# Two decoder layers on one core: normalisation ends written in halves, latent branch tiles first, weight splits inside the first routing unit

## The chip, the core and the metric

The kernel runs on one core of a Trainium2 chip. The metric is the device time in microseconds, the median of the runs. "Span" is the stretch from the first to the last instruction of one profiled execution. TensorE does matmuls into PSUM, VectorE and ScalarE work element by element, GpSimd (POOL) does a few such operations and starts small transfers, and SyncE (SP) starts the large ones.

## The reference, cut to what matters

The input is 256 tokens of width 1024. After an input LayerNorm come two layers:

```python
def hybrid_layer(x, ...):
    c_q, c_kv, k_r, n_q, n_kv, n_gate, m_gate = split(x @ w_in)
    y_mla = mla_attention(q, k, v from c_q, c_kv, k_r) @ w_branch_mla     # 8 heads, latent attention
    y_nsa = nsa_attention(compressed, selected, window) @ w_branch_nsa    # 8 heads in 2 groups
    g_mla, g_nsa = split(sigmoid(m_gate))
    mixed = (g_mla * y_mla + g_nsa * y_nsa) @ w_out
    x = layer_norm(ALPHA * x + mixed, ln1_g, ln1_b)
    x = layer_norm(ALPHA * x + peer(x, ...), ln2_g, ln2_b)
    return x

def peer(x, w_query, sub_keys, expert_u, expert_v):   # 8 heads, two sets of 128 keys, 16384 experts
    q = x @ w_query
    s = q . sub_keys                                   # 8 heads x 2 x 128 scores a token
    sv, si = top_k(s, 16)
    best, pos = top_k(sums of all pairs of sv, 16)     # 16 experts a head and token
    gate = softmax(best)
    return sum over them of gate * gelu(u_e . x) * v_e
```

The kernel computes gelu(u_e . x) for all 128 x 128 experts and multiplies it by a gate that is zero where an expert was not picked.

## The kernel before, in words

**Tiles and splits.** All weights stream through a ring of four slots of 512 KB: 68 tiles of the front part of a layer (T_LAT, T_UQ, T_B, T_UKV, T_MG, T_A, T_BR, T_OUT, T_PQ), 128 tiles of peer_u, 128 of peer_v. SyncE waits for `slot_free` and starts the load (L386, `load`). ScalarE writes the rounded `hi` part of a tile (L477, `split_hi`), VectorE the rest, `lo` (L734, `split_lo`), in place of the raw tile, three tiles ahead of TensorE (AHEAD). Products are made of three matmuls: lo by hi, hi by lo, hi by hi (L1245 to L1247 in `columns_tile`, L1256 in `rows_tile`, L1531 and on for the branch tiles). `tile_step(l, n)` on either engine is the split of tile n + 3.

**Order.** Each engine has its own instruction stream, written out by hand; semaphores order them. The two layers are a loop (`Fori(0, DEPTH)`) on every engine, and the u and v tiles, the query tiles and the gate groups are loops inside it.

**Ends of a sublayer.** `add_and_norm` on VectorE takes the two token tiles in turn: it adds the PSUM result (wide) to ALPHA x (L1067), forms the statistics (L748 to L750), gives the variance to GpSimd, which raises it to the power -1/2 (L427), multiplies (L756), and writes x (L761). TensorE's `transpose_x` (L1274) then transposes x in four groups, two for each token tile, into the two banks of `tr`; `transposed_hi` on ScalarE (L510) and `transposed_lo` on VectorE (L818) split each group. Groups 2 and 3 use the banks of groups 0 and 1 and wait until VectorE has read those. This happens at the start, after each w_out product (LN1), and at the border of the layers. The very first thing on VectorE is the arithmetic of the rotary angles (L768 to L784), whose sines ScalarE makes (L499, L500); after the input normalisation come eight copies into the cos and sin tables (L794 to L801), and four small constants.

**Attention.** Twelve units of four heads each: for each token tile two latent ones, and selected and window for both groups. TensorE runs the scores of unit u+1, a gate tile of the merge gates while there are any, the transposes of the weights of unit u (L1357), and the outputs of unit u-1 (L1504). Outputs go to one of two banks of `acc`, in the order of ATT_ORDER; `copy_o` (L591) and `output_lo` (L1014) split them.

**Branch tiles.** After the last output ScalarE makes four sigmoids of the gates (L631). The eight branch tiles alternate between the latent and the sparse branch for each quarter q of the columns. VectorE multiplies each by its gates (L1046), adds the two (L1054), ScalarE and VectorE split the sum (L638, L1035) into the input of the w_out tiles. Of the eight w_out tiles the last four run for token tile 0 first, then for token tile 1.

**Routing.** `route` is a chain of 14 stages (25 VectorE instructions, L1106 to L1131) that picks the experts of one of 16 units (token tile and head). The splits of the u tiles stand at fixed places in it (`split_after`). Unit 0 runs ahead of the loop with the split of one tile (T_U+3) in it; unit i+1 has the splits of eight tiles.

Of the kernel before, what the change touches and what calls it, by code (L numbers as in the profile page):

```python
# [22 lines left out]
F32 = mybir.dt.float32  # L23
# [9 lines left out]
P = 128  # L33
# [62 lines left out]
    0, 8, 10, 17, 19, 20, 24, 40, 48, 56, 60, 188)  # L96

ATT_ORDER = "F0 F1 O0 F2 O1 F3 O2 F4 F5 O3 F6 F7 O4 O5 O6 O7".split()
O_USE = [A_ATT + ATT_ORDER.index(f"O{k}") for k in range(8)]
MG_USE = [12, 13, 14, 15, 16, 18, 22, 23] + [A_ATT + ATT_ORDER.index(f"F{k}") for k in range(8)]  # L100
# [9 lines left out]
X_XT, X_Q, X_K, X_NQ, X_KT, X_CD, X_HT, X_PC, X_AT, X_XT2, X_PK = 0, 4, 8, 12, 14, 16, 18, 20, 24, 42, 46  # L110
NTR = 48
# [63 lines left out]
def build(nc, t, out):  # L175
    with ExitStack() as ctx:
# [24 lines left out]
        rot = at("rot", [P, TT, ROT, HD], F32, 48 * K)  # L201
        mix = at("mix", [P, 2, 2, 512], F32, 48 * K)
# [91 lines left out]
        ang = at("ang", [P, 4, TT, 48], F32, 0)  # L294
# [33 lines left out]
        x_ready = sem("x_ready")  # L328
        tr_hi = sem("tr_hi")
# [42 lines left out]
        def _(sp):  # L372
# [7 lines left out]
            def load(l, src, first, turns):  # L380
                with sp.Fori(0, turns) as q:
                    for s in range(SLOTS):
                        turn = l * TURNS + (q + first // SLOTS)

                        sp.wait_ge(slot_free[s], OPEN + turn)
                        sp.dma_start(raw[:, s], src[l, q * SLOTS + s]).then_inc(loaded[s], 16)  # L386

            with sp.Fori(0, DEPTH) as l:
                load(l, t["front"], 0, FRONT // SLOTS)
# [5 lines left out]
            sp.wait_ge(stored, 16)  # L395
# [3 lines left out]
        def _(pool):  # L399
# [31 lines left out]
            with pool.Fori(0, DEPTH) as l:  # L431
# [42 lines left out]
        def _(act):  # L474
# [23 lines left out]
            act.wait_ge(angles_ready, 1)  # L498
            nc.scalar.activation(ang[:, 2], ang[:, 0], ACT.Sin).then_inc(sines_ready, 1)  # L499
            nc.scalar.activation(ang[:, 3], ang[:, 1], ACT.Sin).then_inc(sines_ready, 1)  # L500

            with act.Fori(0, DEPTH) as l:
                warm_up(ACT.Gelu, l * 2 + 1)
                for n in range(AHEAD):
                    split_hi(l, 0, n)

                def transposed_hi(first, hi_first, dst):
                    for g in range(4):
                        act.wait_ge(tr_ready, l * NTR + first + g + 1)
                        nc.scalar.activation(dst(g), tr[:, (first + g) % 2].rearrange("p (c t) -> p c t", c=4),  # L510
                                             ACT.Identity).then_inc(tr_hi, 1)
# [5 lines left out]

                transposed_hi(X_XT, 0, xT_part)

# [93 lines left out]

                exp_scores(0)
                for u in range(NU + 1):
                    if u + 1 < NU:
                        exp_scores(u + 1)
# [9 lines left out]
                for b in range(2):  # L627
                    act.wait_ge(acc_read[b], OPEN + l * (NACC // 2) + A_BR // 2)
                g2 = gates[:].rearrange("p (b c) t -> p b c t", b=2)
                for q in range(4):  # L630
                    nc.scalar.activation(g2[:, :, 2 * q:2 * q + 2], g2[:, :, 2 * q:2 * q + 2],  # L631
                                         ACT.Sigmoid).then_inc(gates_ready, 1)
                for q in range(4):
                    for e in range(2):
                        tile_step(l, T_BR + 2 * q + e)
# [4 lines left out]
                for n in range(T_OUT, T_PQ):  # L640
                    tile_step(l, n)

                transposed_hi(X_XT2, 4, xT_part)
# [28 lines left out]
                with act.Fori(0, NKEYS // 8 - 1) as i:  # L672
# [3 lines left out]
                for e in range(8):  # L676
                    gelu_tile(NKEYS // 8 - 1, e)
                    if e == 1:
# [52 lines left out]
        def _(dve):  # L731
# [20 lines left out]
            def normalise(tt, nth, loads, chain, meanwhile=None):  # L752
# [14 lines left out]
            tab = Steps(dve, tables_step, 0, 19)  # L767
            dve.wait_ge(pos_loaded, 32)  # L768
            tab.link(nc.vector.tensor_copy(pos_f[:], pos_i[:]))
            for tt in range(TT):  # L770
                tab.link(nc.vector.tensor_scalar(ang[:, 0, tt], freq[:], pos_f[:, tt:tt + 1], None, ALU.mult))

            tab.link(nc.vector.tensor_scalar(ang[:, 1], ang[:, 0], 1.0 / TWO_PI, None, ALU.mult))
            tab.link(nc.vector.tensor_scalar(ang[:, 1], ang[:, 1], ROUND, None, ALU.add))
            tab.link(nc.vector.tensor_scalar(ang[:, 1], ang[:, 1], ROUND, None, ALU.subtract))
            for part in (PI_A, PI_B, PI_C):
                tab.link(nc.vector.scalar_tensor_tensor(out=ang[:, 0], in0=ang[:, 1], scalar=-part, in1=ang[:, 0],
                                                        op0=ALU.mult, op1=ALU.add))
            tab.link(nc.vector.tensor_scalar(ang[:, 0], ang[:, 0], float(np.float32(np.pi)),
                                             -float(np.float32(np.pi)), ALU.min, ALU.max))  # L780

            tab.link(nc.vector.scalar_tensor_tensor(out=ang[:, 1], in0=ang[:, 0], scalar=-1.0, in1=ang[:, 0],
                                                    op0=ALU.mult, op1=ALU.max))
            nc.vector.tensor_scalar(ang[:, 1], ang[:, 1], -1.0, float(np.pi / 2), ALU.mult, ALU.add).then_inc(angles_ready, 1)  # L784
# [6 lines left out]
            dve.wait_ge(sines_ready, 2)  # L791
            R2, H2 = ROPE // 2, HD // 2

            tab.link(nc.vector.tensor_copy(cos_m[:, :, :R2], ang[:, 3, :, :R2]))  # L794
            tab.link(nc.vector.tensor_copy(cos_m[:, :, R2:], ang[:, 3, :, :R2]))
            tab.link(nc.vector.tensor_copy(sin_m[:, :, R2:], ang[:, 2, :, :R2]))
            tab.link(nc.vector.tensor_scalar(sin_m[:, :, :R2], ang[:, 2, :, :R2], -1.0, None, ALU.mult))
            tab.link(nc.vector.tensor_copy(cos_n[:, :, :H2], ang[:, 3, :, R2:]))
            tab.link(nc.vector.tensor_copy(cos_n[:, :, H2:], ang[:, 3, :, R2:]))
            tab.link(nc.vector.tensor_copy(sin_n[:, :, H2:], ang[:, 2, :, R2:]))  # L800
            tab.link(nc.vector.tensor_scalar(sin_n[:, :, :H2], ang[:, 2, :, R2:], -1.0, None, ALU.mult))  # L801
            tab.end()
# [8 lines left out]
            with dve.Fori(0, DEPTH) as l:  # L811
                st = Steps(dve, dve_step, l * DVE_STEPS, DVE_STEPS)
                split_lo(l, 0, 0)
# [915 lines left out]
```

## Time and profile before

| | |
|---|---|
| median of 3 runs | 2300.91 us (2300.28 to 2303.41) |
| the profiled execution's own time | 2301.64 us |
| its span | 2300.0 us |
| TensorE busy | 2149.0 us, 93% |
| VectorE, ScalarE, GpSimd busy | 1507.9, 1161.5, 177.3 us |
| transfers | 353.47 MB, mean 154 GB/s |
| granted TensorE clock, mean | 0.975 |

In the page's matmul groups durations overlap, since matmuls are pipelined: a 128x256 matmul of 285 ns starts 0.12 us after the one before it. What an engine waited for stands in brackets behind its row, as the idle time before it and what ended that. "issue" there means that the profile shows nothing that released it.

### The profile page before, as it was taken

The numbers are of one execution on the slowest core, as the hardware profiler recorded it, in microseconds if no ns is written. First come the engines' busy times: TensorE is split into PE (matmuls) and PEld (weight loads), VectorE is DVE, ScalarE is ACT, GpSimd is POOL, SyncE is SP. The second block draws the span as 40 slices with busy tenths as digits, with TensorE's granted clock in tenths as the row PEclk, the third lists the DMA queues.
The fourth block names the chain that finished last, engine by engine and source line by source line (L and its number), as shares of the span: only waits on it lengthen the run. The fifth ranks groups of instructions, "written<-read, shape, count | busy, mean of one in ns | idle before, by whom it ended". The sixth has DMA issues, their size and how long they took to land.

```text
span 2300.0 us, 42749 instructions
## 1 busy us (share of the span) xinstructions
PE 2149.0 (93%) x14160; PEld 1928.2 (84%) x14160; DVE 1507.9 (66%) x2784; ACT 1161.5 (50%) x1830; POOL 177.3 (8%) x188
## 2 busy tenths in 40 slices
PE   6988979999999999999988888899999999999997
PEld 5876779999997788788777767899999977887886
DVE  5656657777777855555557557577777687555555
ACT  4445444555557745444444454455545587545543
POOL 2000000000005600000020000000000074000000
PEclk9999989999999999999989999999999999999999
DMA  4622434555551065655546214355555501565554
GB/s 157 226 77 65 154 121 163 181 182 182 181 183 59 13 195 193 196 194 194 169 155 212 76 63 146 130 183 181 182 182 182 174 28 60 193 210 178 194 195 139
DMA packets 96309, 353.47 MB, mean 154 GB/s; under 512 B 11056, under 2 KB 11088, under 8 KB 95856
## 3 DMA queue, kind: packets, MB, share of 16 engines
q1 hardware_dynamic: 94032, 341.90, 45.2%
q0 software_dynamic: 2208, 10.66, 1.4%
q8 instruction: 42, 0.69, 0.1%
q14 instruction: 27, 0.22, 0.0%
HBM read 351.47 MB, written 1.05 MB: 153 GB/s over the span
## 4 chain that ended last, share of the span: by engine, by line
PE 58%; issue 28%; DVE 6%; ACT 4%; POOL 2%; DMA 2%; POOLq 0%; DVEq 0%; ACTq 0%; SPq 0%
PE wide L1256 14%; PE acc L1245 12%; PE acc L1246 12%; PE acc L1247 12%; PE acc L1618 3%; POOL hot_i L463 1%; ACT sc L607 1%; DMA raw<-in_front 1%; ACT hot_i L693 1%; DVE lo L734 1%; ACT hi L477 1%; DVE negmax L987 1%; PE tr L1357 1%; POOL rstd L427 1%; PE acc L1504 1%
## 5 line engine op out<-in xcount | busy, mean ns | idle before, releaser
L734 DVE TENSOR_TENSOR lo<-raw,hi 128x1024 fp32r<-128x1024 f32 x648 | 792.2, 1223 | 589.3 <-ACT hi L477 584.5
L477 ACT ACTIVATE hi<-raw 128x1024 fp32r<-128x1024 f32 x648 | 686.7, 1060 | 520.4 <-DMA raw<-in_peer_v 354.4
L1245 PE MATMUL acc<-xT_hi,lo 128*128 128x256 f32 x2560 | 734.7, 287 | 27.2 <-DVE lo L734 11.2
L1246 PE MATMUL acc<-xT_lo,hi 128*128 128x256 f32 x2560 | 731.1, 286 | 0.0
L1247 PE MATMUL acc<-xT_hi,hi 128*128 128x256 f32 x2560 | 730.8, 285 | 0.0
L1245 PEld LDWEIGHTS acc<-xT_hi,lo 128*128 128x128 f32 x2560 | 498.6, 195 | 32.9 <-DVE lo L734 18.2
L1246 PEld LDWEIGHTS acc<-xT_lo,hi 128*128 128x128 f32 x2560 | 498.7, 195 | 0.1
L1247 PEld LDWEIGHTS acc<-xT_hi,hi 128*128 128x128 f32 x2560 | 498.4, 195 | 0.0
L1256 PE MATMUL wide<-hi,w_lo 128*128 128x512 f32 x1024 | 318.7, 393 | 12.0 <-DVE w_lo L1202 12.0
L1256 PE MATMUL wide<-lo,w_hi 128*128 128x512 f32 x1024 | 316.8, 391 | 0.0
L1256 PE MATMUL wide<-hi,w_hi 128*128 128x512 f32 x1024 | 316.4, 391 | 0.0
L665 ACT ACTIVATE big<-acc 128x256 f32 (+1 forms) x256 | 98.6, 385 | 345.5 <-PE acc L1247 345.5
L1256 PEld LDWEIGHTS wide<-hi,w_lo 128*128 128x128 f32 x1024 | 192.8, 189 | 54.5 <-DVE lo L734 10.9
L1256 PEld LDWEIGHTS wide<-lo,w_hi 128*128 128x128 f32 x1024 | 193.6, 189 | 40.9
L1256 PEld LDWEIGHTS wide<-hi,w_hi 128*128 128x128 f32 x1024 | 193.1, 189 | 40.2
L463 POOL TENSOR_TENSOR hot_i<-iota,picksT 128x512 f32<-128x512 f32 x128 | 133.1, 1041 | 866.3 <-PE acc L1247 835.3
L1618 PEld LDWEIGHTS acc<-hot_j,hot_i 128*128 128x128 f32 x1024 | 128.2, 196 | 38.1 <-ACT hot_i L693 27.8
L1618 PE MATMUL acc<-hot_j,hot_i 128*128 128x128 f32 x1024 | 145.6, 287 | 10.5 <-ACT hot_i L693 8.3
L1202 DVE TENSOR_TENSOR w_lo<-big,w_hi 128x256 fp32r<-128x256 f32 x256 | 106.8, 418 | 1.1 <-ACT w_hi L713 1.1
L713 ACT ACTIVATE w_hi<-big 128x256 fp32r (+1 forms) x256 | 102.2, 400 | 2.7 <-DVE big L1185 2.7
L1185 DVE TENSOR_TENSOR big<-acc,big 128x512 f32 (+1 forms) x128 | 87.6, 684 | 14.5 <-PE acc L1618 13.6
L693 ACT ACTIVATE hot_i<-hot_i,ones 128x512 f32<-128x512 f32 x128 | 90.2, 706 | 0.0
(259 smaller groups left out, 1790.0 us busy)
## 6 DMA issues: line engine op xcount, KB each, us to landing
raw<-in_peer_u SPq DMA_DIRECT2D x256, 512.0 KB, 3.3
raw<-in_peer_v SPq DMA_DIRECT2D x256, 512.0 KB, 3.3
raw<-in_front SPq DMA_DIRECT2D x136, 512.0 KB, 3.6
ln_par<-in_ln POOLq DMA_DIRECT2D x10, 512.0 KB, 5.8
w<-in_cmp_w POOLq DMA_DIRECT2D x2, 2048.0 KB, 8.9
xs<-in_x SPq DMA_DIRECT2D x2, 512.0 KB, 7.2
keys<-in_sub_keys POOLq DMA_DIRECT2D x2, 512.0 KB, 4.0
out<-xs SPq DMA_DIRECT2D x1, 1024.0 KB, 3.9
```

The lines of the kernel that those rows point to most:

```text
L463: nc.gpsimd.tensor_tensor(hot_i[:, e], iota[:].unsqueeze(1).broadcast_to([P, 4, P]), toks, ALU.subtract).then_inc(differences_ready, 1)
L477: nc.scalar.activation(hi[:, s], raw[:, s], ACT.Identity).then_inc(hi_done, 1)
L665: nc.scalar.activation(big[:, i * 2 + e // JB, :, e % JB], acc[:, e % 2, :SEQ].rearrange("p (g t) -> p g t", t=TB), ACT.Gelu).then_inc(acc ...
L693: nc.scalar.activation(hot_i[:, e], hot_i[:, e], ACT.Relu, bias=ones[:, 0:1], scale=-1.0).then_inc(hot_i_ready, 1)
L713: nc.scalar.activation(w_hi[:, s].rearrange("p (g t) -> p g t", t=TB), big[:, i + c // JB, :, c % JB], ACT.Identity).then_inc(w_hi_done, 1)
L734: nc.vector.tensor_tensor(lo[:, s], raw[:, s], hi[:, s].bitcast(F32), ALU.subtract).then_inc(lo_done, 1)
L1202: nc.vector.tensor_tensor(w_lo[:, s].rearrange("p (g t) -> p g t", t=TB), big[:, i + c // JB, :, c % JB], part, ALU.subtract).then_inc(w_l ...
L1245: mm(dst, lo[:, s, c], xh[:, k], start=k == 0, stop=False)
L1246: mm(dst, hi[:, s, c], xl[:, k], start=False, stop=False)
L1247: ins = mm(dst, hi[:, s, c], xh[:, k], start=False, stop=k == DK - 1)
L1256: ins = mm(wide[:, tt, 512 * h:512 * h + width], a[:, tok], w[:, s, off:off + width], start=first and k == 0, stop=last and k == 2)
L1618: ins = mm(acc[:, e % 2, r * P:(r + 1) * P], hot_i[:, e, r], hot_j[:, e, r], start=True, stop=True)
```

## The change

On all engines the loop over the layers is written out (`for l in range(DEPTH)`). The edits, in order of the kernel:

- The first token tile's groups still go to `tr`; the second's go to `wide[:, 0]`, under two new semaphores. x is written in two halves, each with its own signal, and each group is transposed from its half. In `add_and_norm` the lo part of group 0 stands between the two steps of the second token tile's normalisation; at the border of the layers too.
- The angle arithmetic moves from VectorE's start to behind the first three splits of layer 0, and the table copies behind the third split of the query projection. The input is the first thing that VectorE works on.
- The output is stored in three parts: token tile 0, and the two halves of token tile 1.
- The branch tiles come as four latent ones (`y_mla` holds their gated results) and four sparse ones; the first latent one stands inside the last attention unit, ahead of its transposes. ScalarE makes the sigmoids in four steps around the last unit.
- In the routing the split of T_U+3 stands ahead of unit 0, and those of T_U+4 and T_U+5 inside it; the later units' splits move on by two tiles, and so do the steps at the end of the u tiles.

```diff
-ATT_ORDER = "F0 F1 O0 F2 O1 F3 O2 F4 F5 O3 F6 F7 O4 O5 O6 O7".split()
+ATT_ORDER = "F0 F1 O0 F2 O1 F3 O2 F4 F5 O3 F6 F7 O4 O5 O6 M0 O7".split()
...
-            sp.wait_ge(x_ready, TT * (1 + 2 * DEPTH))
-            sp.dma_start(out, xs[:]).then_inc(stored, 16)
+            sp.wait_ge(x_ready, last + 2)
+            sp.dma_start(out[:, 0], xs[:, 0]).then_inc(stored, 16)
+            for c in range(2):
+                sp.wait_ge(x_ready, last + 2 + c + 1)
+                sp.dma_start(out[:, 1, 512 * c:512 * c + 512], xs[:, 1, 512 * c:512 * c + 512]).then_inc(stored, 16)
...
@@ ScalarE
+                    if u == NU - 1:
+                        branch_gates(0)
+                    if u == NU:
+                        branch_gates(1)
+                        tile_step(l, T_BR)
...
+                branch_gates(2)
+                branch_gates(3)
+                for c in range(1, 4):
+                    tile_step(l, T_BR + c)
                 for q in range(4):
+                    tile_step(l, T_BR + 4 + q)
                     act.wait_ge(mix_sum, l * 4 + q + 1)
...
@@ VectorE
-                nc.vector.scalar_tensor_tensor(out=xs[:, tt], in0=xs[:, tt], scalar=rstd[:, tt:tt + 1],
-                                               in1=ln_par[:, 1], op0=ALU.mult, op1=ALU.add).then_inc(x_ready, 1)
+                for c in range(2):
+                    half = slice(512 * c, 512 * c + 512)
+                    nc.vector.scalar_tensor_tensor(out=xs[:, tt, half], in0=xs[:, tt, half], scalar=rstd[:, tt:tt + 1],
+                                                   in1=ln_par[:, 1, half], op0=ALU.mult, op1=ALU.add).then_inc(x_ready, 1)
...
+                branch_out(0, y_mla[:, 0])
                 output_lo(7)
+                for c in range(1, 4):
+                    branch_out(c, y_mla[:, c])
...
                 for q in range(4):
+                    branch_out(4 + q, mix[:, q % 2, 1])
+                    if q > 0:
+                        mixed_lo(q - 1)
+                    nc.vector.tensor_tensor(mix[:, q % 2, 0], y_mla[:, q], mix[:, q % 2, 1], ALU.add).then_inc(mix_sum, 1)
...
-                add_and_norm(0, T_PQ - 1, W_OUT, R_LN1, l * 64 + 64, lambda: tile_step(l, T_PQ - AHEAD))
-                transposed_lo(X_XT2, 4, x_part(xT_hi), x_part(xT_lo))
+                add_and_norm(0, T_PQ - 1, W_OUT, R_LN1, l * 64 + 64, lambda: transposed_lo(l, 1, 0))
+                transposed_lo(l, 1, 1)
+                tile_step(l, T_PQ - AHEAD)
+                transposed_lo(l, 1, 2)
+                transposed_lo(l, 1, 3)
...
-                route(0, 0, range(1))
+                after_route(0, 0)
+                route(0, 0, (1, 2))
                 with dve.Fori(0, NKEYS // 8 - 1) as i:
-                    route(i + 1, i, range(1, 9))
+                    route(i + 1, i, range(3, 11))
...
@@ TensorE
                     if u + 1 < NU:
                         scores(u + 1)
+                    else:
+                        outputs_read(4)
+                        outputs_read(5)
+                        branch_tile(0)
...
                 outputs(NU - 1)
...
+                for c in range(1, N_BR):
+                    if c == 4:
+                        outputs_read(6)
+                        outputs_read(7)
+                    branch_tile(c)
```

`branch_out(c, dst)` on VectorE waits for tile c and its gates, writes the product to dst and splits tile c + 3 of the branch tiles; `outputs_read(k)` waits until VectorE has split output k; `branch_tile(c)` is the old body of 24 matmuls.

## Rows read from the trace of the kernel before

**Rows 1.** The page's part 1: busy time, share of the span, instructions.

```profile
PE 2149.0 (93%) x14160; PEld 1928.2 (84%) x14160; DVE 1507.9 (66%) x2784; ACT 1161.5 (50%) x1830; POOL 177.3 (8%) x188
```

**Rows 2.** TensorE's waits: who waited <- for whom: us, times, longest.

```profile
PE tr L1274 <- DVE xT_lo L818: 28.2, 4, 8.6
...
PE acc L1245 <- DVE lo L734: 11.2, 2, 5.6
```

**Rows 3.** Timeline, the start: start us, duration us, instruction [idle before <- releaser].

```profile
18.60 0.17 DVE L794 COPY cos_m<-ang 128x32 f32<-128x32 f32 x1
...
20.91 1.22 DVE L734 TENSOR_TENSOR lo<-raw,hi 128x1024 fp32r<-128x1024 f32 x1
22.04 1.28 DVE L818 TENSOR_TENSOR xT_lo<-tr,xT_hi 128x512 fp32r<-128x512 f32 x2
...
26.44 0.58 PE L1245 MATMUL acc<-xT_hi,lo 128*128 128x256 f32 x1 [1.69 <-DVE xT_lo L818]
```

**Rows 4.** Timeline, LN1 of layer 0.

```profile
290.71 1.23 DVE L734 TENSOR_TENSOR lo<-raw,hi 128x1024 fp32r<-128x1024 f32 x1
...
295.57 0.69 DVE L818 TENSOR_TENSOR xT_lo<-tr,xT_hi 128x512 fp32r<-128x512 f32 x1 [1.24 <-ACT xT_hi L510]
...
297.69 0.58 PE L1245 MATMUL acc<-xT_hi,lo 128*128 128x256 f32 x1 [1.94 <-DVE xT_lo L818]
```

**Rows 5.** Timeline, the border of the layers.

```profile
1156.08 1.52 POOL L427 TENSOR_TENSOR rstd<-var,neg_half 128x1 f32<-128x1 f32 x1 [4.62 <-DVE var L754]
...
1160.82 1.22 DVE L734 TENSOR_TENSOR lo<-raw,hi 128x1024 fp32r<-128x1024 f32 x1 [1.90 <-issue]
...
1166.37 0.58 PE L1245 MATMUL acc<-xT_hi,lo 128*128 128x256 f32 x1 [1.70 <-DVE xT_lo L818]
```

**Rows 6.** Transfers by line: count, KB each, median us from issue to landing.

```profile
raw<-in_front SPq DMA_DIRECT2D x136, 512.0 KB, 3.6
...
out<-xs SPq DMA_DIRECT2D x1, 1024.0 KB, 3.9
...
lat_g<-in_lat_g POOLq DMA_DIRECT2D x2, 4.0 KB, 2.1
```

**Rows 7.** Timeline, the last attention unit of layer 0 and the first branch tile.

```profile
231.95 1.06 PE L1357 MATMUL tr<-ident,sc 128*128 128x128 f32 x8 [3.10 <-DVE sc L1000]
...
238.00 1.28 ACT L631 ACT_TABLE_LOAD   x1 [0.54 <-DVE oT_lo L1014]
238.11 0.38 PE L1531 MATMUL acc<-oT_hi,lo 128*128 128x256 f32 x1 [1.07 <-issue]
239.29 3.90 ACT L631 ACTIVATE gates<-gates 128x1024 f32<-128x1024 f32 x4
```

**Rows 8.** Windows: busy us by engine; then granted clock, DMA share, GB/s.

```profile
136.00:139.50 3.50, 3.50 (x34) 3.46 (x33) 0.99 (x1) 0.19 (x1) 0.00 (x0) 1.00 0.12 47
234.00:237.00 3.00, 3.00 (x16) 1.29 (x12) 0.00 (x0) 0.00 (x0) 0.00 (x0) 0.50 0.00 0
937.00:940.60 3.60, 3.60 (x11) 2.81 (x10) 3.55 (x6) 1.91 (x4) 0.00 (x0) 0.54 0.02 9
```

**Rows 9.** Timeline, branch and w_out tiles of layer 0.

```profile
264.96 0.68 DVE L1054 TENSOR_TENSOR mix<-mix 128x512 f32<-128x512 f32 x1
...
267.29 1.22 DVE L734 TENSOR_TENSOR lo<-raw,hi 128x1024 fp32r<-128x1024 f32 x1 [1.65 <-ACT hi L477]
...
278.36 0.72 PE L1256 MATMUL wide<-hi,xT_lo 128*128 128x512 f32 x2 [1.25 <-DVE lo L734]
```

**Rows 10.** Timeline of the first routing unit, and a window behind it.

```profile
329.67 0.29 DVE L1106 COPY r_s<-scr 128x256 f32<-128x256 f32 x1 [0.27 <-DVE scr L1083]
...
344.72 1.20 DVE L734 TENSOR_TENSOR lo<-raw,hi 128x1024 fp32r<-128x1024 f32 x1
...
345.98 0.58 PE L1245 MATMUL acc<-xT_hi,lo 128*128 128x256 f32 x1 [5.62 <-DVE lo L734]
...
346.00:349.60 3.60, 3.60 (x17) 3.60 (x18) 3.45 (x16) 0.00 (x0) 0.00 (x0) 0.50 0.02 5
```

More of the change, by code:

```diff
@@ L378, in _, with load @@
                 sp.dma_start(xs[:, tt], t["x"][:, tt]).then_inc(x_loaded[tt], 16)
-            def load(l, src, first, turns):
+            def load(l, src, first, turns, skip=0):
                 with sp.Fori(0, turns) as q:
@@ L430, in _ @@
                 rsqrt(tt, tt, tt + 1)
-            with pool.Fori(0, DEPTH) as l:
+            for l in range(DEPTH):
                 pool.wait_ge(slot_free[SLOTS - 1], OPEN + l * TURNS)
@@ L497, in _, with transposed_hi @@
             nc.scalar.activation(causal_r[:], causal[:], ACT.Identity).then_inc(masks_ready, 1)
[L498 to L502, printed above, removed]
+            for l in range(DEPTH):
                 warm_up(ACT.Gelu, l * 2 + 1)
[L504 to L510, printed above, removed]
+                def transposed_hi(first, tt, dst):
+                    for cg in range(2):
+                        if tt == 0:
+                            act.wait_ge(tr_ready, l * NTR + first + cg + 1)
+                            src = tr[:, cg]
+                        else:
+                            act.wait_ge(wide_x_ready, l * 4 + (2 if first == X_XT2 else 0) + cg + 1)
+                            src = wide[:, 0, 512 * cg:512 * cg + 512]
+                        nc.scalar.activation(dst(2 * tt + cg), src.rearrange("p (c t) -> p c t", c=4),
                                              ACT.Identity).then_inc(tr_hi, 1)
@@ L670, in after_gelu @@
                     split_hi(l, (i * 2 + n // SLOTS), n % SLOTS)
-                with act.Fori(0, NKEYS // 8 - 1) as i:
+                after_gelu(0, 0)
+                for e in range(8):
+                    gelu_tile(0, e)
+                    if e > 0:
+                        after_gelu(0, e)
+                with act.Fori(1, NKEYS // 8 - 1) as i:
                     for e in range(8):
@@ L1133, in route @@
                     assert sum(map(len, stages)) == ROUTE_STEPS
-                    split_after = [round((len(stages) - 1) * (e + 0.5) / 8) for e in range(8)]
+                    split_after = [round((len(stages) - 1) * (e + 0.5) / len(splits)) for e in range(len(splits))]
                     for g, stage in enumerate(stages):
@@ L1217, in _ @@
                 split_w_lo(0, NKEYS - 1, SLOTS - 1)
-                add_and_norm(1, NT - 1, W_V, R_LN2, l * 64 + 96)
+                add_and_norm(1, NT - 1, W_V, R_LN2, l * 64 + 96,
+                             (lambda: transposed_lo(l + 1, 0, 0)) if l + 1 < DEPTH else None)
                 st.end()
@@ L1506, in outputs, with branch_tile, outputs_read @@
                         ins.then_inc(acc_ready, 1)
+                def branch_tile(c):
+                    n, bank = T_BR + c, BR_USE[c] % 2
+                    s = n % SLOTS
+                    acc_free(l, BR_USE[c])
+                    tile_ready(l, n // SLOTS, s)
+                    for f in range(2):
+                        for k in range(4):
+                            w = slice(k * 256 + f * P, k * 256 + f * P + P)
+                            dst = acc[:, bank, f * SEQ:(f + 1) * SEQ]
+                            mm(dst, lo[:, s, w], oT_hi[:, c // 4, k], start=k == 0, stop=False)
+                            mm(dst, hi[:, s, w], oT_lo[:, c // 4, k], start=False, stop=False)
+                            ins = mm(dst, hi[:, s, w], oT_hi[:, c // 4, k], start=False, stop=k == 3)
+                    ins.then_inc(slot_free[s], 1)
+                def outputs_read(oi):
+                    use = O_USE[oi]
+                    pe_.wait_ge(acc_read[use % 2], OPEN + l * (NACC // 2) + use // 2 + 1)
                 scores(0)
@@ L1511, in _ @@
                         scores(u + 1)
+                    else:
+                        outputs_read(4)
+                        outputs_read(5)
+                        branch_tile(0)
                     if u + 8 < N_MG:
```

224 lines of the change are left out of this document (117 added, 107 removed).

## The prediction

> **What bounds the kernel now.** I read the page first: TensorE is busy 93% of the span [rows 1], so time can only come out of its idle stretches, or of stretches at half clock. The table of waits names the idle ones: the largest is TensorE's transposes of x held by VectorE's xT_lo (28.2 us in 4 waits), and two waits of 5.6 us for a weight split make up the 11.2 us of L1245 on L734 [rows 2]. Then I went through the timeline stage by stage: the start, the two ends of the mixing sublayer (LN1), the border of the layers, the last attention unit, the branch tiles, the first routing unit, the end. In each the reader is to see what VectorE does while TensorE waits, since that engine writes what TensorE waits for. The long loops over u and v tiles show no such waits and the change leaves them as they are.
>
> **Part 1, the normalisation ends.** The change gives the second token tile's transposes their own PSUM banks (wide), so they no longer wait until VectorE has read the first tile's; it moves the lo parts of the first token tile ahead; and it writes x in halves.
>
> *Start.* Before, the 8 table copies run from 18.60 to 20.37, then 4 small constants, a split at 20.91, two xT_lo from 22.04, then a hole until the second tile's transposes and hi parts come, two more xT_lo, and the first real matmul at 26.44 [rows 3]. After, the copies are gone from here (1.8) and the hole closes, because the second tile's transposes run while VectorE works on the first. VectorE then does, from the end of the second normalisation (18.67, earlier by up to 0.4 as the angle arithmetic no longer stands ahead of the statistics; I take 0.2): constants 0.55, two lo parts 1.28, a split 1.13, two lo parts 1.28, and TensorE starts 0.3 later: 18.5+0.55+1.28+1.13+1.28+0.3 = 23.0. Gain 3.4. The angle arithmetic (3.1 us of VectorE) now stands behind the first splits, beside the first weight tile, which takes 5.5 us at the start; if it were late, ScalarE's squares would slip and the spare accumulator bank gives 2.9 us more. The table copies move into the query projection, where the splits feed TensorE closely: I charge 0.3 (0 to 1.8). Net 3.1.
>
> *LN1, two layers.* Before: split at 290.71, then x, then four lo parts with a hole of 1.24 between them, the matmul at 297.69 [rows 4]. After, VectorE has no hole: lo part from 290.71 (0.60), two half writes 1.24, a lo part 0.60, the split 1.14, two lo parts 1.25, and the 0.6 to the matmul as before: 296.15. Gain 1.5 each, 3.0.
>
> *Border of the layers.* Before, after the loop's jump VectorE has 1.90 us of idle time that nothing releases, then the split at 1160.82, and the matmul comes at 1166.37 [rows 5]. After, with the layers written out, no jump; the first lo part fills the wait for rstd (ready at 1157.60 [rows 5]): x written 1158.0 to 1159.2, lo 0.6, split 1.14, two lo 1.25, 0.35: 1162.6. Gain 3.8.
>
> Rule of the Trainium skill beside it: "Runtime: NRT & Kernel Launch", section Instruction fetch mechanics, says that instructions are prefetched only straight ahead and that a taken branch to a page outside the window waits for a fetch. The 1.90 us agrees; by that rule nothing else is lost in writing out, and the sum stays.
>
> *The end.* One 1 MB store lands 3.9 us after its issue; a 4 KB transfer takes 2.1 [rows 6]. The last store after the change is 256 KB: a quarter of the way between, about 2.6. Gain 1.3 (0 to 1.8).
>
> Sum of part 1: 3.1+3.0+3.8+1.3 = 11.2.
>
> **Part 2, the branch tiles.** Before, TensorE idles 3.10 us ahead of the last unit's transposes (3.32 in layer 1), and the first branch tile starts at 238.11, 1.07 after the last output matmul, because it waits for that output's lo part [rows 7]. A branch tile is 24 matmuls at 0.12, 2.88 us. The one put inside the last unit fits the hole: its weights were split long before (by 214), its bank is free and the two outputs that it reads are done. The next three need only the latent branch, so the 1.07 goes too.
>
> The hole also costs afterwards. TensorE's granted clock is 0.50 from 233.8 to 237.1 (a row of [rows 8]), that is 1.2 instead of 2.4 GHz, just behind the 3.1 us of idle; it happens in both layers. All output matmuls of the last two units lie in it and take twice the time. With the hole filled I expect full clock: 3.0 us become 1.5. Both ends for this: 0 if the clock falls all the same, 1.6 if not. I take 1.5, since elsewhere TensorE at full work keeps 1.00.
>
> ScalarE must now load the sigmoid's table and do one gate before its share of pT: load 1.28, gate 0.98 (3.90 for 4) [rows 7], from 230.9 to 233.2; its pT copy then ends at 233.8 instead of 233.2. The outputs of unit 11 start after 234.4. Hidden. The Trainium skill, "ScalarE: Activation LUTs", section What ACT_TABLE_LOAD costs, adds a drain of about 1.4 us to each load; by it the copy would end at 235.1 and some 0.7 us per layer would be lost; here the sigmoid starts 1.29 after its load, so the sum goes without.
>
> So tile 1 starts at about 235.5, tile 4 ends at 247.0 (call it t).
>
> What is late next: the second half. The four sparse tiles come every 2.88, but each needs from VectorE a product, a split, a lo part and a sum, and these hang in one chain with ScalarE: from a sum at 264.96 over ScalarE's hi part and split to VectorE's split at 267.29 [rows 9] are 2.33, then 1.14 for it (the spacing of a split and what follows [rows 3]), 0.61 for the lo part, and the next sum: 4.08 a round. Before there was one round for two tiles (5.76). The first sum waits for the split of the tile whose slot tile 3 frees at t-2.9: load 3.6 [rows 6] with some waiting 3.8, hi 1.06, lo 1.13, so t+3.1; the fourth sum is t+15.3, and the split behind it, for output tile 3, is ready 3.5 later, t+18.8, where TensorE wants it at t+16.8. The loss is 2.1. Output tile 7 follows 8.9 behind tile 3, as before (269.4 to 278.36), since its slot comes free by tile 3: t+27.9 = 274.9 against 278.36 [rows 9]. Gain 3.45; in layer 1 the half-clock stretch is 0.3 shorter and the same sum gives 3.2. Part 2: 6.65. The bounds: with loads of 4.6 us (the longest here) 1 less per layer, without the clock's share 1.5 less.
>
> **Part 3, the first routing unit.** Before, route 0 runs from 329.67 to 343.6 with a single split in it; the second comes at 344.72 and TensorE idles 5.62 us until 345.98, then runs at 0.50 until 349.8, which costs another 2 [rows 10]. After: split of u tile 3 at 330.4 to 331.5; stages 0 to 3, 3.0; split of tile 4, ready 337.6 (wanted 340.4); stages 4 to 10, 4.7; split of tile 5, ready 343.5 (wanted 343.2, late 0.3); stages 11 to 13 and the first two of unit 1, 3.8; split of tile 6, ready 348.4 (wanted 346.4, late 2.0). From then on each split comes in time, as the steady loop has 17 us of VectorE work in 23. Stall 2.3 instead of 5.6: gain 3.3 a layer, 6.6. Behind a wait of 2 us in the v loop the clock was down for 3.6 us too [rows 8], so I leave the clock's 2 us as they are; if the clock stays up, 2 more per layer. The tail runs two tiles later against TensorE but keeps its order; the picks are copied some 7 us before they are wanted: nothing.
>
> **Sum.** 11.2+6.65+6.6 = 24.4 us off the profiled execution's 2301.64 (span 2300.0 and 1.64 around it): 2277.2. The median before is 0.7 lower than that execution: 2276.5.
>
> **Rivals.**
> 1. *Clock stays down in the last unit* and the chain of sums is as long as computed: 3.0 less, and longer loads 1 more: gain 20.5, 2280. For it: the clock fell in the v loop as well, behind a wait of 2 us and with TensorE at full work [rows 8]. Against it: the half clock of 234 to 237 has no other cause in sight. Chance 0.17.
> 2. *Clock stays up in the routing stage*, the stall being shorter: 4.0 more, 2272.5. For it: behind the wait of 2.3 us at 134 it stayed at 1.00 [rows 8]. Against: in the v loop it did not. Chance 0.22.
> 3. *Covered elsewhere:* TensorE's earlier work runs into loads, since the ring of 4 slots ties each split to the release 6 us before it; part 2 gives nothing and part 1 half: gain 12, 2289. Against it: DMA share is 0.5 and the loads are tied to releases, which move along. Chance 0.07.
> 4. *Slower:* writing both layers out makes each engine stream more distinct code, and a stream that runs dry costs what the jump costs now, 1.90 us. It decides from 13 such misses on the path; with 20 the time is 2301+38-24 = 2315. Against it: the layer's straight code is already streamed twice, with no unexplained stall but the one. Chance 0.03.
> The forecast has 0.51.
>
> **Range and chances.** 2270 to 2284 takes in the forecast, rivals 1 and 2 and the unknown ends above. A measurement of this kernel tells 0.2% (4.6 us) from no change: faster 0.94, same 0.03, slower 0.03.
>
> **What would show it.** First weight matmul at about 23; 1.5 between LN1's old and new place; no idle "issue" at VectorE at the border; a branch tile ahead of the last unit's transposes, granted clock 1.00 over them and the outputs; waits of TensorE for splits of about 2 us at output tiles 2 and 3; in the first routing unit a wait of about 2 us at tile 6 and none of 5.6. I am wrong if new idle of TensorE appears where none was, or if the time is above 2290.

## The result, and the profile after

The changed kernel takes 2270.74 us (median of 4 runs, 2268.11 to 2280.07) where the kernel before takes 2301.26 beside it (2300.28 to 2303.41). The ratio is 0.9879, 95% interval 0.9855 to 0.9903: 30.5 us less by the medians. The forecast was 2276.5, 24.4 less, with a range of 2270 to 2284. Direction and range held; the middle was 5.8 too high, and the time lies 0.7 above the low end of the range. The same kernel timed once more, as the control below, takes 2268.16, just under it. The profiled execution took 2271.67 us.

The page of the changed kernel, span and busy time (before: [rows 1]):

```profile
span 2269.9 us, 41699 instructions
...
PE 2145.3 (95%) x14160; PEld 1926.3 (85%) x14160; DVE 1509.6 (67%) x2794; ACT 1160.2 (51%) x1829; POOL 172.4 (8%) x188
```

TensorE's busy time is only 3.7 us lower; 26 of the 30 us came out of its idle time. Its waits (who waited <- for whom: us, times, longest):

```profile
PE wide L1337 <- DVE xs L802: 18.0, 4, 5.1
...
PE wide L1312 <- DVE lo L773: 10.3, 9, 2.0
PE acc L1695 <- ACT hot_i L732: 7.6, 2, 3.8
...
PE acc L1301 <- DVE lo L773: 3.6, 4, 1.6
```

Of the 28.2 us on xT_lo [rows 2] the first row is what is left (the second tile's transposes wait for x itself), and the 11.2 us of the routing unit's split are 3.6. The second row is mostly w_out tiles that wait for their splits. The third, the first gate group of each layer, waited 3.88 us before as well and was no part of the prediction; it comes back below.

**Where the 30.1 us of span came from.** I laid TensorE's rows of both traces side by side. The same matmul starts earlier after the change, and by how much is what has been gained up to there; what this grows by from one matmul to a later one is what the stretch between them gave.

| stretch | forecast | measured |
|---|---|---|
| start, to the first weight matmul | 3.4 | 3.6 |
| branch tiles, layers 0 and 1, from the last but two unit's transposes | 3.45, 3.2 | 2.6, 3.5 |
| LN1, two layers (1.4 in layer 0, layer 1 taken as the same) | 3.0 | 2.8 |
| routing, layers 0 and 1, first score matmul to the first gate matmul | 3.3, 3.3 | 5.3, 5.1 |
| border of the layers | 3.8 | 3.9 |
| end | 1.3 | 1.5 |
| all other stages together | -0.3 | 1.8 |

The last row is what is left of larger pieces, none of them forecast. The v loops gave 3.7 and 2.45, where stretches of half clock at 936.9 and 2073.5 (3.4 us long each) have no counterpart after the change and the waits ahead of them are shorter. The stages from the border to the last but two unit of layer 1 took 4.5 back, with 10.2 us more at half clock. That these nearly cancel is luck. In layer 1 the LN1 stretch by itself gave 0.6 in this trace, as half clock lies at its head; in the kernel with part 1 alone it gave 1.4 in both layers.

The start, LN1, the border and the end, on the timeline (start us, duration us, instruction [idle before <- releaser]; compare [rows 3 to 5]):

```profile
22.88 0.55 PE L1301 MATMUL acc<-xT_hi,lo 128*128 128x256 f32 x1 [2.91 <-issue]
...
284.04 0.69 DVE L831 TENSOR_TENSOR xT_lo<-tr,xT_hi 128x512 fp32r<-128x512 f32 x1
284.64 1.40 DVE L802 SCALAR_TENSOR_TENSOR xs<-xs,rstd,ln_par 128x512 f32<-128x512 f32 x2
...
286.57 1.21 DVE L773 TENSOR_TENSOR lo<-raw,hi 128x1024 fp32r<-128x1024 f32 x1
...
289.58 0.57 PE L1301 MATMUL acc<-xT_hi,lo 128*128 128x256 f32 x1 [2.17 <-DVE xT_lo L831]
...
1143.32 1.97 PE L1337 MATMUL wide<-ident,xs 128*128 128x128 f32 x8 [5.05 <-DVE xs L802]
...
1147.06 0.55 PE L1301 MATMUL acc<-xT_hi,lo 128*128 128x256 f32 x1 [1.77 <-issue]
```

The reader is to see that VectorE has no hole left between the first lo part and the matmul, neither in LN1 nor at the border. The stores (the page's part 6; us from issue to landing): the last two, half a token tile each, land 2.2 us after their issue, where the interpolation said 2.6:

```profile
out<-xs SPq DMA_DIRECT2D x1, 512.0 KB, 2.6
out<-xs SPq DMA_DIRECT2D x2, 256.0 KB, 2.2
```

The last attention unit of layer 0 (compare [rows 7]), then a window over it (us; busy by engine; granted clock, DMA share, GB/s):

```profile
226.10 1.28 ACT L638 ACT_TABLE_LOAD   x1
227.40 1.06 ACT L638 ACTIVATE gates<-gates 128x1024 f32<-128x1024 f32 x1
227.67 1.03 PE L1421 MATMUL tr<-ident,sc 128*128 128x128 f32 x8
...
234.26 0.69 DVE L1068 TENSOR_TENSOR y_mla<-acc,gates 128x512 f32<-128x512 f32 x1 [1.84 <-PE acc L1584]
```

```profile
230.00:237.00 7.00, 7.00 (x61) 6.40 (x58) 3.41 (x5) 4.05 (x5) 1.04 (x2) 1.00 0.60 241
```

The first sigmoid starts 1.30 after its table load does, as the one before the change had 1.29, and pT (ScalarE's copy of the transposed weights, which the outputs read) is in time. (The Trainium skill, "ScalarE: Activation LUTs", section What ACT_TABLE_LOAD costs, adds a drain of 1.4 us to the 1.28; the trace doesn't agree: neither the first ACTIVATE behind the load nor the load itself, which starts 0.02 behind the instruction ahead of it, shows such a time.) The transposes wait for nothing, and the outputs run at a granted clock of 1.00, the 2.4 GHz level, where [rows 8] had 0.50. Behind it the chain of sums, with TensorE's waits for the w_out splits:

```profile
246.75 0.68 DVE L1105 TENSOR_TENSOR mix<-y_mla,mix 128x512 f32<-128x512 f32 x1
...
250.82 0.68 DVE L1105 TENSOR_TENSOR mix<-y_mla,mix 128x512 f32<-128x512 f32 x1
...
254.90 0.68 DVE L1105 TENSOR_TENSOR mix<-y_mla,mix 128x512 f32<-128x512 f32 x1
...
258.60 0.70 PE L1312 MATMUL wide<-hi,xT_lo 128*128 128x512 f32 x2 [1.07 <-DVE lo L773]
258.97 0.68 DVE L1105 TENSOR_TENSOR mix<-y_mla,mix 128x512 f32<-128x512 f32 x1
...
262.67 0.70 PE L1312 MATMUL wide<-hi,xT_lo 128*128 128x512 f32 x2 [1.07 <-DVE lo L773]
...
271.65 0.70 PE L1312 MATMUL wide<-hi,xT_lo 128*128 128x512 f32 x2 [1.91 <-DVE lo L773]
```

The sums are 4.08 us apart, three times: the round of the forecast to the second decimal. Their matmuls belong to w_out tiles 2, 3 and 7. Last, the first routing unit (compare [rows 10]) and a window from 334 to 356, of the changed kernel and then of the kernel before:

```profile
336.07 0.39 PE L1301 MATMUL acc<-xT_hi,lo 128*128 128x256 f32 x1 [0.24 <-DVE lo L773]
...
340.76 0.39 PE L1301 MATMUL acc<-xT_hi,lo 128*128 128x256 f32 x1 [1.56 <-DVE lo L773]
...
334.00:356.00 22.00, 20.20 (x167) 19.80 (x166) 18.73 (x49) 9.65 (x14) 0.00 (x0) 1.00 0.50 168
```

```profile
334.00:356.00 22.00, 16.39 (x123) 16.18 (x122) 17.96 (x62) 7.11 (x10) 0.00 (x0) 0.84 0.38 121
```

The stall of 5.62 us is now waits of 0.24 and 1.56, and the clock stays at 1.00. The forecast had kept the half clock.

### The profile page after: what moved, and what is told of

Its sections match the earlier page's. It is cut to its first block, busy times and chain, and to the rows that moved or that the text cites. A ratio compares the mean times of both kernels' runs of the same rounds, so it can differ in the third digit from the quotient of the medians.

```text
span 2269.9 us, 41699 instructions
## 1 busy us (share of the span) xinstructions
PE 2145.3 (95%) x14160; PEld 1926.3 (85%) x14160; DVE 1509.6 (67%) x2794; ACT 1160.2 (51%) x1829; POOL 172.4 (8%) x188
## 4 chain that ended last, share of the span: by engine, by line
PE 80%; DVE 8%; ACT 4%; DMA 3%; issue 3%; POOL 1%; POOLq 0%; DVEq 0%; ACTq 0%; SPq 0%
PE wide L1312 33%; PE acc L1301 13%; PE acc L1302 12%; PE acc L1303 12%; PE acc L1695 4%; DVE lo L773 2%; DMA raw<-in_front 2%; ACT hi L491 1%; ACT sc L628 1%; DMA raw<-in_peer_v 1%; POOL hot_i L477 1%; PE wide L1664 1%; DVE negmax L1032 1%; DMA raw<-in_peer_u 1%; ACT hot_i L732 1%
## 5 line engine op out<-in xcount | busy, mean ns | idle before, releaser
L1232 DVE SCALAR_TENSOR_TENSOR hot_j<-wide,picksT 128x512 f32<-128x512 f32 x128 | 86.6, 679 | 6.2 <-PE acc L1303 6.2
```

## The experiments

Each was timed in five rounds against the kernel before, on the same chip. Ratios are to that, with their 95% interval; 0.001 is 2.3 us. Each letter in the expectations names one explanation and the time that it would give.

**One part at a time: the loops over the layers.** The kernel before with one edit on every engine:

```diff
-            with dve.Fori(0, DEPTH) as l:
+            for l in range(DEPTH):
```

> Kernel before with only the loop over the two layers written out on all engines. Theory A (each part of the change gains at its own place, and what came on top of the forecast is stretches of half clock that fell away): 1.9 us less at the border of the layers, where VectorE waited 1.90 us for nothing that the profile shows, so 2299.4 against 2301.3. Rival B (writing out is what gave the 6 us on top, as constants take the place of register sums ahead of each wait): 2293 to 2295.

Measured: 2295.8 us (2291.04 to 2299.0), ratio 0.998 (0.9968 to 0.9992), 2 to 7 us less. The border of its trace, against [rows 5]:

```profile
1151.69 1.28 DVE L761 SCALAR_TENSOR_TENSOR xs<-xs,rstd,ln_par 128x1024 f32<-128x1024 f32 x1 [0.52 <-POOL rstd L427]
1152.89 1.22 DVE L734 TENSOR_TENSOR lo<-raw,hi 128x1024 fp32r<-128x1024 f32 x1
...
1158.26 0.55 PE L1245 MATMUL acc<-xT_hi,lo 128*128 128x256 f32 x1 [1.46 <-DVE xT_lo L818]
```

The 1.90 us of "issue" between x and the split are gone. From the last wait of the v loop to this matmul it takes 19.4 us, before 21.5: the border gave 2.1. The Trainium skill, "Runtime: NRT & Kernel Launch", section Instruction fetch mechanics, says that a taken branch out of the prefetched code waits for a fetch. The trace fits it, in that the 1.90 us are gone with the jump; a fetch itself is not shown. The other 6.0 us of its profiled execution had been gained by then in stages without such a jump: two half-clock stretches of the trace of before, at 90 to 94 and 936 to 941, are missing here, 1.7 us each, and the v loop's first wait is 0.85 us instead of 2.06; 1.4 stay without a place. So the size lies nearer B, but for a reason that neither theory had.

**The routing alone.** The kernel before with the splits of the first unit as in the change:

```diff
-                route(0, 0, range(1))
+                after_route(0, 0)
+                route(0, 0, (1, 2))
```

> Kernel before with the routing edit alone (the split of u tile 3 ahead of unit 0, those of tiles 4 and 5 inside it, the later ones moved on). Theory A: two waits of 5.6 us become 0.3 and 1.6 in each layer, and no half clock follows, which gave 2 us: 2 x 5.3 = 10.6 less, 2290.7. Rival C (the clock staying up in the changed kernel was luck of where the stretch fell): 2 x 3.3 = 6.6 less, 2294.7, with a granted clock of 0.50 for some 4 us behind the wait of 1.6 us.

Measured: 2291.84 us (2287.98 to 2292.42), ratio 0.995 (0.9937 to 0.9962), 9 to 15 us less; the forecast for this part was 6.6. From the first score matmul of the routing to the first gate matmul, layer 0, it takes 388.7 us in the kernel before, 388.8, 388.7 and 389.0 in the three experiments that keep the old splits (layers written out, branch tiles alone, part 1 alone), 383.3 here and 383.4 in the changed kernel. Its window:

```profile
334.00:356.00 22.00, 20.26 (x167) 19.85 (x166) 17.75 (x55) 9.55 (x14) 0.00 (x0) 1.00 0.48 165
```

The clock is up here as well. So the 5.3 us belong to this part whatever else is in the kernel. Of the stall 3.8 are gone in the changed kernel (5.62 less 0.24 and 1.56); the rest, 1.5, I put down to the clock.

**The branch tiles alone.** The kernel before with the new order, the sigmoids and M0 in the last unit:

```diff
-ATT_ORDER = "F0 F1 O0 F2 O1 F3 O2 F4 F5 O3 F6 F7 O4 O5 O6 O7".split()
+ATT_ORDER = "F0 F1 O0 F2 O1 F3 O2 F4 F5 O3 F6 F7 O4 O5 O6 M0 O7".split()
```

> Kernel before with the branch edit alone (latent tiles first, one ahead of the last unit's transposes). Theory A: 2.9 for the tile in the hole, 1.1 for the wait before the first tile, 1.5 for the clock, less about 3 for the chain of sums: 2.4 to 3.4 a layer, 5 to 7 in all, 2294 to 2296, granted clock 1.00 over the last unit's outputs. Rival C: the half clock behind the hole stays: 2297 to 2299.

Measured: 2296.05 us (2285.68 to 2298.5), ratio 0.996 (0.9944 to 0.9977), 5 to 13 us less, forecast 6.65. In its trace the stretch from the last but two unit's transposes to the matmul behind LN1 is 2.8 us shorter than before in layer 0 and 4.3 in layer 1. The median is A's and the ratio is below both, and in both layers no half clock follows the last unit's transposes, so C, the clock staying down, is refuted by the trace. The runs spread by 13 us, so the times alone would not settle it.

**The hole left open.** The changed kernel with M0 behind the outputs of the last unit:

```diff
-                    else:
-                        outputs_read(4)
-                        outputs_read(5)
-                        branch_tile(0)
...
-                for c in range(1, N_BR):
+                for c in range(N_BR):
```

> Changed kernel with the first latent tile behind the last unit's outputs again, all else as changed. Theory A: the hole of 3.1 us comes back and with it a stretch of 0.50 of the clock over the outputs; 2.9 and 1.5 us lost in each layer: 2270.7 + 8.8 = 2279.5. Rival C (the clock does not follow the hole): 2270.7 + 5.8 = 2276.5. Rival D (the chain of sums sets the time of the stage whatever TensorE does before it, since its start waits for a load): 2270.7 to 2272.

Measured: 2279.91 us (2277.17 to 2289.62), ratio 0.9915 (0.9898 to 0.9932), 8.3 us more than the changed kernel by the two ratios (11.3 more than the control), and the value of A. Its trace:

```profile
224.78 1.07 PE L1421 MATMUL tr<-ident,sc 128*128 128x128 f32 x8 [3.14 <-DVE sc L1045]
```

```profile
226.00:230.00 4.00, 4.00 (x21) 1.85 (x18) 0.58 (x1) 2.56 (x5) 0.00 (x0) 0.57 0.01 4
```

The wait is back and the half clock behind it too. From the last but two unit's transposes to LN1's matmul the open hole costs 5.7 us in layer 0 and 4.7 in layer 1, where the forecast put 2.9 for the tile and 1.5 for the clock, 4.4. That the filled hole keeps the clock up is shown, here and by the other traces: all seven with the tile in the hole have no half clock between the last unit's transposes and the branch tiles, in either layer; all five with the hole open have it in both. It lasted 3.4 us in three of the five and 10.2 in two (routing alone, part 1 alone), so its price varies.

**Interleaved branch tiles.** The changed kernel with two branch tiles between most sums:

```diff
+BR_ORDER = [0, 1, 4, 2, 5, 3, 6, 7]
...
-                    e, q = divmod(c, 4)
+                    e, q = divmod(BR_ORDER[p], 4)
```

> The changed kernel with its eight branch tiles in the order M0 M1 S0 M2 S1 M3 S2 S3 (M of the latent branch, S of the sparse one), so that most sums lie two tiles of 2.88 us apart instead of one. Theory A (the chain of sums, 4.08 us a round, is what makes TensorE wait 3.1 us per layer behind the branch tiles): of the waits of 0.27, 1.07, 1.07 and 0.7 us only about 0.5 us is left; 2.5 us less per layer, 2265.5 to 2266.5 us against 2270.7 for the changed kernel. Theory B (the waits come from the weight tiles of w_out landing late, whatever the order of the sums): the waits stay, 2270 to 2272 us.

The changed kernel once more on the same chip, the control for this and the next two:

> The changed kernel itself, as the one that the other three are compared with on the same chip: 2270.7 us if the chip is like the first; its runs spread by 12 us so far, and theory F (half-clock stretches of TensorE whose places and number differ from run to run make that spread) expects again single runs from 2268 to 2280 us, and a profile whose stretches lie partly at other times than in the first one.

Measured: the control 2268.16 us (2264.74 to 2273.67, a spread of 9), ratio 0.9866 (0.9838 to 0.9894); interleaved 2266.8 us (2262.97 to 2270.76), ratio 0.9849 (0.9818 to 0.988). The intervals overlap, so the times alone show no gain. The waits do, in layer 0 of the interleaved kernel:

```profile
260.03 0.70 PE L1314 MATMUL wide<-hi,xT_lo 128*128 128x512 f32 x2 [0.92 <-DVE lo L774]
...
269.05 0.70 PE L1314 MATMUL wide<-hi,xT_lo 128*128 128x512 f32 x2 [1.98 <-DVE lo L774]
```

One wait is left of the two or three. The last sums still follow each other at 4.08 (S2 and S3 are neighbours in this order). The stretch to LN1 is 2.1 us shorter than the control's in layer 0 and 0.9 in layer 1, against 2.5 each by A; B, no change, fails on the waits. The wait of tile 7 stays in every order.

**Three splits in the first routing unit.** The changed kernel with

```diff
-                route(0, 0, (1, 2))
+                route(0, 0, (1, 2, 3), (3, 9, 12))
...
-                    if e == 6:
+                    if e == 7:
                         pe_.wait_ge(whole_ready, 4 + l + 1)
```

(the later units' splits and the steps at the end of the u tiles one tile on).

> The changed kernel with three weight splits inside the first routing unit (behind its stages 3, 9 and 12) instead of two. Theory A (the waits of 0.24 and 1.56 us that TensorE still has there are only the place of VectorE's splits): both go, and 1.5 us per layer with them: 2267.5 us. Theory E (VectorE has no time to spare over the whole routing stretch, and the last picks come later): the same time comes back as a wait ahead of the gates or of the v loop: 2270.5 to 2272 us.

Measured: 2260.07 us (2256.67 to 2263.63), ratio 0.9826 (0.98 to 0.9853): 9.2 us less than the control by the ratios, where A gave 3 and E none. Both sizes are wrong. The waits in the unit are gone as A said, but another went with them. First the changed kernel at its first gate group, then this one:

```profile
689.98 0.39 PE L1664 MATMUL wide<-next_b,places_b 128*128 128x512 bf16 x1
...
695.71 0.38 ACT L699 ACTIVATE big<-acc 128x256 f32<-128x256 f32 x1 [4.01 <-PE acc L1303]
...
696.10 4.03 POOL L477 TENSOR_TENSOR hot_i<-iota,picksT 128x512 f32<-128x512 f32 x4 [411.69 <-PE acc L1303]
...
699.47 2.08 PE L1695 MATMUL acc<-hot_j,hot_i 128*128 128x128 f32 x8 [3.80 <-ACT hot_i L732]
```

```profile
689.43 0.39 PE L1663 MATMUL wide<-next_b,places_b 128*128 128x512 bf16 x1
...
690.02 4.03 POOL L477 TENSOR_TENSOR hot_i<-iota,picksT 128x512 f32<-128x512 f32 x4 [406.67 <-PE acc L1302]
...
693.39 1.16 PE L1694 MATMUL acc<-hot_j,hot_i 128*128 128x128 f32 x8 [1.33 <-ACT hot_i L732]
```

GpSimd waits for the last u tile, then takes 3.4 us with ScalarE until the gates can start. In the changed kernel, and before it, TensorE does the eight bf16 distance matmuls (2.56 us) ahead of the last u tile and then idles. My edit had moved them behind it by moving the whole tail one tile, and they now fill the wait. I had not seen that when I wrote the expectation.

**The distance matmuls alone moved.** The changed kernel with

```diff
-                    if e == 6:
+                    if e == 7:
                         pe_.wait_ge(whole_ready, 4 + l + 1)
```

> The changed kernel with one thing moved: TensorE's eight bf16 matmuls that form the distances of the first gate group stand behind the last u tile instead of ahead of it (the splits of the first routing unit stay two). GpSimd's first difference of a layer waits for that last tile, and in the changed kernel TensorE then idles 3.8 us until ScalarE has made the first hot_i. Theory A (this order is where most of the three-split kernel's gain came from): the wait falls to 1.3 us, 2.5 us less per layer, and up to 1.7 more in a layer where the half-clock stretch behind it goes: 2262 to 2264 us where the changed kernel takes 2268.2. Theory B (the gain came from the third split): no more than 1 us in all, 2267 to 2268 us.

Measured, on another chip than the control: 2263.46 us (2260.05 to 2277.93), ratio 0.9854 (0.9831 to 0.9878). In its trace:

```profile
1817.80 1.16 PE L1695 MATMUL acc<-hot_j,hot_i 128*128 128x128 f32 x8 [1.32 <-ACT hot_i L732]
```

The wait fell from 3.78 to 1.32, and from the first score matmul to the first v tile it takes 2.3 us less than the control in layer 0 and 3.3 in layer 1: A, by the trace. The run times (2.8 us below the control by the ratios) don't settle it. The same two stretches are 5.9 and 4.2 us shorter with the three splits, so about half of that kernel's gain is this order and half the splits with their clock.

**Both together.** The interleaved order and the three splits:

> The interleaved branch order and the three splits together. If both gains are real and lie in different stretches they add: 2262 to 2263.5 us. If one of them is covered by the other rival: 2266 to 2268 us.

Measured: 2256.99 us (2250.08 to 2258.5), ratio 0.9801 (0.9773 to 0.9829): 43 us below the kernel before and 11 below the control. It is lower than expected, as the three splits brought 9.2 where A had given them 3. Its median is below that of the three splits alone (2260.07), but the intervals of the two ratios overlap and the spans of the two traces, 2255.3 and 2255.9, are alike: that the interleaved order adds to the splits is not shown.

**Part 1 alone.** The kernel before with the written-out layers and all the normalisation ends, old branch tiles and old routing:

```diff
-            sp.wait_ge(x_ready, TT * (1 + 2 * DEPTH))
-            sp.dma_start(out, xs[:]).then_inc(stored, 16)
+            for c in range(2):
+                sp.wait_ge(x_ready, last + 2 + c + 1)
...
+                        src = wide[:, 0, 512 * cg:512 * cg + 512]
```

> The kernel before with part 1 alone: layers written out, second token tile's transposes in their own banks, x in halves, angle arithmetic and table copies moved, the store in three parts; branch tiles and routing as before. Theory A (the prediction's terms 3.1, 3.0, 3.8 and 1.3 hold): 11.2 us less than before, 2289 to 2290 us. Theory G (the 5.5 us that writing out the layers gave by itself are more than the 1.9 us of the jump, because half-clock stretches went elsewhere, and come on top of the other terms): 14 to 16 us less, 2285 to 2287 us.

Measured: 2291.06 us (2282.67 to 2299.47), ratio 0.9966 (0.9951 to 0.9981), 4 to 11 us less. G is out, A is at the edge. In its trace LN1 gave 1.4 in each layer and the border 3.9, as forecast; the start gave 2.7. The profiled execution was the slowest of the ten and shows one thing that no other trace here has. Layer 1, a 2 MB load, then a weight split on ScalarE and VectorE, and TensorE:

```profile
1210.32 0.59 POOL L451 DMA_DIRECT2D w<-in_cmp_w  x1 [15.45 <-PE wide L1281]
...
1220.11 1.06 ACT L483 ACTIVATE hi<-raw 128x1024 fp32r<-128x1024 f32 x1 [6.68 <-DMA raw<-in_front]
...
1221.20 1.23 DVE L749 TENSOR_TENSOR lo<-raw,hi 128x1024 fp32r<-128x1024 f32 x1 [5.72 <-ACT hi L483]
...
1223.00 0.74 DVE L913 TENSOR_SCALAR v_mla<-wide,rstd 128x512 f32<-128x512 f32 x1
...
1223.85 1.19 PE L1281 MATMUL wide<-hi,xT_lo 128*128 128x512 f32 x2 [7.96 <-issue]
```

TensorE idles 7.96 us here, where it waits 1.4 to 2.5 in the other 23 cases, both layers of all twelve traces. What it wants had been split in time; it waits in `wide_free(l, W_A)` until VectorE has read `wide` for v_mla (1223.00 to 1223.74). VectorE does that behind the split of a later tile, that split waits for ScalarE's hi part, and ScalarE waits for the raw tile. SyncE had issued that tile's load at 1210.20, 0.1 us before GpSimd's 2 MB load, and it took 9.9 us; in the 23 other cases the load at this place took 3.3 to 4.1. The clock is at 0.50 from 1218.8 on for 10.2 us. So this is a late load and not rival 4, code that comes late; why this one load was late in this execution stays open. (The load behind it, issued with the 2 MB load under way, took 6.6 to 9.5 in those 23 cases and 8.9 here.)

The ratios of the three parts alone, 0.9966, 0.996 and 0.995, multiply to 0.9877; the whole has 0.9879. The parts add, as far as times can tell: by their intervals the product is good to some 6 us, and the whole to 5.5, so an overlap of a few us would not be seen.

## Why the prediction was right, and where it was off

**Part 1, 11.2.** Start, LN1, border and end came within 0.2 us each of their terms by the trace, 11.8 in all, with LN1 counted at its 1.4 in layer 1 too, where half clock took 0.8 of it. The start varies by itself: the traces with the old one have the first weight matmul at 26.3 to 27.1, those with the new one at 22.6 to 23.8. The reading of VectorE's row as one gapless list of known durations was enough. The run times of part 1 alone give 8 (4 to 11), lower but not in conflict.

**Part 2, 6.65, measured 6.1.** The tile in the hole, the clock behind it (1.6 us by the trace: 4.3 gained at the transposes, 5.9 at the last output) and the 1.07 came as forecast, and so did the period of the sums. The loss behind it was sized too small: 3.1 instead of 2.1. The step that was short is "so t+3.1" for the first sum: it came at t+4.0, because the raw tile of the last branch tile landed 4.6 us after its slot was free, where the sum had 3.8. The two ln_par loads that GpSimd had started at 231.47 and 231.98 were not beside it any more, as they had landed by 236.9. The three raw loads from 234.26 on, the first of them still beside these two, are 2.88 apart and took 4.24, 4.20 and 4.47 us, so that each began before the one ahead had landed; with the hole open the second of them starts 3.9 behind the first, and the later ones took 3.4. That the delay was handed on in this way is my reading and not shown by itself. The forecast's bound of 1 us for long loads covers it. The waits stand at w_out tiles 2 and 3 and at tile 7, as said. The 3.5 of layer 1 is close to the forecast's 3.2 by luck: 1.6 of it lie ahead of the last unit, where half clock lasted 6.8 us before and 3.4 after, and 0.8 were lost again behind tile 7; without both it is 2.7, like layer 0. (The prediction's t+27.9 for tile 7 is 0.2 more than its own terms, 18.8 and 8.9, give.)

**Part 3, 6.6, measured 10.4.** This is the main miss. The stall: 0.24 and 1.56 against 0.3 and 2.0, right in place and 0.5 too long. The failed step is "so I leave the clock's 2 us as they are". Rival 2 (0.22) was the truth: behind waits of 0.24 and 1.56 us the clock stays up, which gave 1.5 a layer where the rival had 2. That is seen at this place in all eight traces with the new splits, while the four with the old ones (before, layers written out, branch alone, part 1 alone) have half clock there. I had leaned on the v loop's stretch [rows 8], and that one is no fixed thing: in layer 0 it comes behind waits of 2.06 (before) and 2.00 (the control), not behind 1.54 to 1.75 (distances moved, after, three splits), and not behind 2.39 either (part 1 alone, branch tiles alone). Behind the first gates the layers part again: half clock lasts 6.8 us there in layer 0 where it was 3.4, and layer 0 loses 1.0; it lasts 3.4 in layer 1 where it was 6.8, and layer 1 gains 1.1. No step of mine was about these.

**The clock as a whole.** Adding windows of 1 us, TensorE had 77.1 us of work at half clock in the trace of before and 65.0 in that of after; the difference is worth 6.0 us. The control, the same kernel as after, had 58.9, so a single trace of it is good to some 3 us in this. The stretches behind the last unit and the first routing unit, both layers, held 14.0 of the 77.1 and are all gone; the others changed place and gave back 1.9.

**The rivals.** 1 (clock down in the last unit) is refuted by the window at 230 and by the seven traces with the hole filled. 3 (covered elsewhere) would have left a gain of 12; 22 to 33 by the ratio's interval refute it. 4 (slower by code) is refuted in size: the kernel with only the layers written out is 2 to 7 us faster.

## What to carry to other kernels

Write the busiest helper engine's instructions behind the last wait as a gapless list: where the list is gapless the sum holds to 0.2 us, and what it misses is the clock behind the stall, which was worth 1.9 us behind 5.62 of stall and went with it here. When a stall is taken out, look at what TensorE does ahead of the next dependent wait: independent work that stands before the releasing instruction can stand behind it, as the eight distance matmuls showed.

## What the runs showed of the hardware

Which waits bring half clock is not fixed: the same kernel, at the same place of layer 1, behind the same wait, in two executions (the changed kernel, then the control):

```profile
1253.46 5.32 PE L1449 MATMUL acc<-w,blk 128*30 128x128 f32 x32 [2.30 <-issue]
```

```profile
1252.15 3.65 PE L1449 MATMUL acc<-w,blk 128*30 128x128 f32 x32 [2.31 <-issue]
```

The first ran into half clock and the second did not. Such stretches make a part of the spread of 12 us between runs of one kernel, and they are why a difference of 2 or 3 us could be read from the stretches of a trace but not from five rounds of times. What decides it stays open.
